# Block attention of a hybrid mixer, its units' scores and values' products issued in pairs

## What is computed

```python
u_conf, u_sc, u_att, u_lru = jnp.split(rms_norm(x, g) @ w_in, splits, axis=-1)
y_a = conformer_conv_mixer(u_conf, ...)   # depthwise convolution of 31 taps, group norm
y_b = short_conv_mixer(u_sc, ...)
y_c = moba_attention(u_att)               # block attention, the part that is reordered
y_d = rglru_mixer(u_lru, ...)             # convolution of 4 taps, two gates, a scan
y = jnp.concatenate([y_a, y_b, y_c, y_d], axis=-1) @ w_out
```

## Time and profile before

| | |
|---|---|
| time of three runs | 1281.03, 1281.20, 1281.74 us; median 1281.2 |
| profiled execution | 1281.13 us |
| its span on the core | 1279.3 us (1.8 us lie outside of it) |
| PE busy | 1271.2 us, 99% |
| DVE, ACT busy | 740.7 us (58%), 569.1 us (44%) |
| chain that ended last | PE 92%, DVE 4%, ACT 2% |

### The profile page before, as it was taken

One profiled execution on the slowest core, in us unless ns is written; L12 is line 12 of the kernel. 1 busy time (PEld: TensorE's weight loads), 2 busy tenths in 40 slices (PEclk: granted clock), 3 DMA queues, 4 the chain that ended last, 5 costly groups with the idle time before them and its releaser, 6 DMA issues.

```text
span 1279.3 us, 15979 instructions
## 1 busy us (share of the span) xinstructions
PE 1271.2 (99%) x6406; PEld 1065.5 (83%) x6406; DVE 740.7 (58%) x1091; ACT 569.1 (44%) x974; POOL 7.0 (1%) x8
## 2 busy tenths in 40 slices
PE   9999999999999999999999999999999999999998
PEld 9877898898888888888888898778898888888886
DVE  5779687575576555555633489777653433433333
ACT  4566554344446444444422364576442422322222
POOL 0000011000000000000000000000000000000000
PEclk9999999999999999999999999999999999999999
DMA  8445446222224233333433143123243333333311
GB/s 259 138 149 164 164 133 193 104 67 67 89 92 144 92 94 99 99 99 99 148 98 99 34 153 99 50 67 115 74 141 99 94 94 94 115 99 99 99 50 66
DMA packets 43521, 138.54 MB, mean 108 GB/s; under 512 B 4628, under 2 KB 10260, under 8 KB 43192
## 3 DMA queue, kind: packets, MB, share of 16 engines
q1 hardware_dynamic: 43016, 137.13, 34.2%
q10 hardware_dynamic: 432, 0.39, 0.1%
HBM read 131.74 MB, written 5.77 MB: 107 GB/s over the span
## 4 chain that ended last, share of the span: by engine, by line
PE 92%; DVE 4%; ACT 2%; DMA 1%; issue 1%; DVEq 0%; SPq 0%
PE bank L1285 16%; PE bank L1286 16%; PE bank L1287 16%; PE bank L1426 5%; PE bank L1427 5%; PE bank L1429 5%; PE bank L1430 5%; PE bank L1428 5%; PE bank L1431 5%; PE bank L1505 1%; DVE wlo L2153 1%; DVE R L2302 1%; PE bank L1357 1%; PE bank L1368 1%; DVE gb L2292 1%
## 5 line engine op out<-in xcount | busy, mean ns | idle before, releaser
L1285 PE MATMUL bank<-xh,whi 128*128 128x512 f32 (+1 forms) x1136 | 414.6, 365 | 1.0 <-DVE xl L2179 0.9
L1286 PE MATMUL bank<-xl,whi 128*128 128x512 f32 (+1 forms) x1136 | 409.9, 361 | 0.0
L1287 PE MATMUL bank<-xh,wlo 128*128 128x512 f32 (+1 forms) x1136 | 409.9, 361 | 0.0
L2153 DVE TENSOR_TENSOR wlo<-stage,whi 128x1024 fp32r<-128x1024 f32 (+1 forms) x222 | 267.4, 1210 | 227.9 <-ACT whi L1688 227.6
L1688 ACT CAST whi<-stage 128x1024 fp32r<-128x1024 f32 (+1 forms) x222 | 228.5, 1036 | 201.1 <-PE bank L1431 157.2
L1285 PEld LDWEIGHTS bank<-xh,whi 128*128 128x128 f32 x1136 | 214.4, 189 | 40.8 <-issue 7.0
L1287 PEld LDWEIGHTS bank<-xh,wlo 128*128 128x128 f32 x1136 | 214.4, 189 | 32.5
L1286 PEld LDWEIGHTS bank<-xl,whi 128*128 128x128 f32 x1136 | 214.5, 189 | 31.8 <-issue 0.2
L1426 PE MATMUL bank<-whi,xh 128*128 128x512 f32 x281 | 110.3, 393 | 0.1
L1427 PE MATMUL bank<-whi,xh 128*128 128x512 f32 x281 | 109.4, 389 | 0.0
L1431 PE MATMUL bank<-whi,xl 128*128 128x512 f32 x281 | 109.4, 389 | 0.0
(11 more groups left out here) (339 smaller groups left out, 1406.1 us busy)
## 6 DMA issues: line engine op xcount, KB each, us to landing
stage<-in_W_m SPq DMA_DIRECT2D x64, 512.0 KB, 3.6
stage<-in_W_up SPq DMA_DIRECT2D x44, 512.0 KB, 3.6
stage<-in_W_down SPq DMA_DIRECT2D x22, 512.0 KB, 3.6
stage<-in_W_in_a SPq DMA_DIRECT2D x19, 512.0 KB, 4.0
stage<-in_W_out SPq DMA_DIRECT2D x16, 512.0 KB, 3.7
stage<-in_W_in_b SPq DMA_DIRECT2D x10, 512.0 KB, 3.6
stage<-in_W_kv_k SPq DMA_DIRECT2D x8, 512.0 KB, 3.7
stage<-in_W_kv_v SPq DMA_DIRECT2D x8, 512.0 KB, 3.9
```

The costliest lines, as they stand in the source:

```text
L1285: e.matmul(b[:, cols], hi[:, k, :], xh[:, k, cols], start=(k == 0), stop=False)
L1286: e.matmul(b[:, cols], hi[:, k, :], xl[:, k, cols], start=False, stop=False)
L1287: last = e.matmul(b[:, cols], lo[:, k, :], xh[:, k, cols], start=False, stop=(k == 7))
L2153: e.tensor_tensor(wlo[:, plan.place[i], c], stage[:, i % NSTAGE, c], whi[:, plan.place[i], c].bitcast(F32), ALU.subtract).then_inc(S["w_lo"])
```

## The change

Units go in pairs (0 and 1, 2 and 3, 4 and 5, 6 and 7). `mb_scores(u)` issues the scores of u and u + 1 one behind the other; the values' products of a pair are issued together, directly ahead of the next pair's scores. The step that DVE and ACT shared under the name `mb_score` is two now, `mb_logit` (DVE) and `mb_exp` (ACT), so that they can stand at different places of the list. Each step of a pair has its own place: logits of u, logits of u + 1 with the exponential of u, reciprocal and scaling of u with the exponential of u + 1, turn of u with the scaling of u + 1, turn of u + 1, values' products. The taps are given out in other portions, 60 as before. No arithmetic is changed, and no instruction is added or removed. The core of the diff:

```diff
-    def mb_score(self, u):
-        for e in range(2):
-            self.fill("mb_score", u, e)
-            self.out(("mb_score", u, e), "mb_logit", 2 * u + e + 1)
-        self.step("mb_score", u)
+    def mb_scores(self, u):
+        for v in (u, u + 1):
+            for e in range(2):
+                self.fill("mb_score", v, e)
+                self.out(("mb_score", v, e), "mb_logit", 2 * v + e + 1)
+            self.step("mb_score", v)
+        self.step("mb_logit", u)
...
+        self.mb_pv(0)
+        self.mb_pv(1)
+        self.mb_scores(2)
+        tap(1)
+        yield
+        self.step("mb_logit", 3)
+        self.step("mb_exp", 2)
+        tap(3)
+        yield
+        self.step("mb_norm", 2)
+        self.step("mb_exp", 3)
+        tap(3)
+        yield
+        self.mb_turn(2)
+        self.step("mb_norm", 3)
+        tap(3)
+        yield
+        self.mb_turn(3)
+        tap(3)
+        yield
+
+        self.mb_pv(2)
+        self.mb_pv(3)
+        self.mb_scores(4)
+        tap(1)
+        yield
+        self.step("mb_logit", 5)
+        self.step("mb_exp", 4)
         tap(2)
         yield
+
+        self.step("mb_norm", 4)
+        self.step("mb_exp", 5)
+        self.lru_gates(0)
         tap(3)
         yield
...
+        self.mb_turn(4)
+        self.step("mb_norm", 5)
+        tap(3)
+        yield
+        self.mb_turn(5)
+        tap(3)
+        yield
+
+        self.mb_pv(4)
+        self.mb_pv(5)
+        self.mb_scores(6)
...
-            def mb_score(u):
+            def mb_exp(u):
...
-            def mb_score(u):
+            def mb_logit(u):
```

More of the change, by code:

```diff
@@ L813, in beside_mixer_two @@
         yield
-        self.mb_score(0)
+        self.mb_scores(0)
+        tap(1)
+        yield
+        self.step("mb_logit", 1)
+        self.step("mb_exp", 0)
         tap(2)
         yield
-        tap(3)
-        yield
         self.step("mb_norm", 0)
-        self.mb_score(1)
-        tap(2)
-        yield
+        self.step("mb_exp", 1)
         tap(3)
@@ L828, in beside_mixer_two @@
         self.step("mb_norm", 1)
-        self.mb_score(2)
-        tap(2)
+        tap(3)
         yield
+        self.mb_turn(1)
+        tap(3)
[7 more added lines that the diff above has]
+        self.step("mb_exp", 2)
         tap(3)
@@ L834, in beside_mixer_two @@
         self.step("mb_norm", 2)
[L835 to L838, removed]
+        self.step("mb_exp", 3)
+        tap(3)
         yield
-        tap(4)
+        self.mb_turn(2)
+        self.step("mb_norm", 3)
+        tap(3)
         yield
[L843 to L846, removed]
+        self.mb_turn(3)
[4 more added lines that the diff above has]
+        self.mb_scores(4)
+        tap(1)
+        yield
+        self.step("mb_logit", 5)
+        self.step("mb_exp", 4)
         tap(2)
@@ L849, in beside_mixer_two @@
         self.step("mb_norm", 4)
+        self.step("mb_exp", 5)
[4 more added lines that the diff above has]
+        self.step("mb_norm", 5)
+        tap(3)
+        yield
+        self.mb_turn(5)
+        tap(3)
+        yield
+        self.mb_pv(4)
+        self.mb_pv(5)
+        self.mb_scores(6)
         tap(1)
         yield
[L852 to L866, removed]
+        self.step("mb_logit", 7)
+        self.step("mb_exp", 6)
+        self.lru_gates(1)
         tap(3)
@@ L869, in beside_mixer_two @@
         self.step("mb_norm", 6)
-        self.mb_turn(5)
-        self.mb_pv(4)
-        self.mb_score(7)
+        self.step("mb_exp", 7)
         tap(3)
         yield
+        self.mb_turn(6)
+        self.step("mb_norm", 7)
+        self.step("lru_a")
         tap(3)
         yield
[L878 to L886, removed]
         self.mb_turn(7)
-        self.step("lru_a")
-        tap(4)
-        yield
         tap(60)
@@ L897, in beside_mixer_two @@
         yield
+        self.mb_pv(6)
         self.mb_pv(7)
@@ L2129, in _ @@
                         cf_var=cf_var, cf_exp=cf_exp, cf_gate=cf_gate, in2_a=in2_a, in2_v=in2_v,
-                        mb_score=mb_score, mb_norm=mb_norm, mb_turn=mb_turn, lru_in=lru_in, lru_gate=lru_gate,
+                        mb_exp=mb_exp, mb_norm=mb_norm, mb_turn=mb_turn, lru_in=lru_in, lru_gate=lru_gate,
                         lru_a=lru_a, lru_b=lru_b, lru_gelu=lru_gelu, sc_c=sc_c, sc_conv=sc_conv,
@@ L2704, in _ @@
                         last_norm=last_norm, cf_in=cf_in, cf_tap=cf_tap, cf_parts=cf_parts, cf_mean=cf_mean, cf_scale=cf_scale,
-                        cf_out=cf_out, mb_score=mb_score, mb_norm=mb_norm, mb_pv=mb_pv, lru_in=lru_in, lru_a=lru_a,
+                        cf_out=cf_out, mb_logit=mb_logit, mb_norm=mb_norm, mb_pv=mb_pv, lru_in=lru_in, lru_a=lru_a,
                         lru_b=lru_b, lru_scan=lru_scan, sc_x=sc_x, sc_conv=sc_conv, sc_b=sc_b, post_norm=post_norm,
```

## The result

The changed kernel takes 1282.85 us (median of 22 runs), the kernel before 1281.22 (22 runs beside them): ratio 1.0012, 95% interval 1.0007 to 1.0018. One run of the 22, at 1581 us and a mean granted clock of 0.75, stands apart and is left out of the ratio. The change costs 1.6 us, which is under the 0.2% that the prediction set for telling a change from none, though the interval excludes 1.

A forecast was written before the change was run, and what follows sets the result against it. PE, busy 99% of the span, was taken to bound the kernel. From 1281.13 us, 2.8 saved on stretches and waits of 2.8, 0.8 and 0.6 added gave 1282.5 us; range 1280.0 to 1284.9.

The forecast's parts named there:

- A: The forecast's own case: gain taken back by three waits, 1280.8 to 1283.7 us, no measurable change; chance 0.67.
- fewer stretches: Half-array stretches on PE in the block attention fall from twelve (5.3 us) to five (2.5 us), saving 2.8 us.
- idle ahead of unit 4's turn: PE asks at 21.4 us, but VectorE's queue delays unit 4's reciprocal and scaling until 24.1; PE waits 2.8 us.
- rival D: Granted clock falls to 1.2 GHz behind the idle; each 8 products cost 1.8 us more, 1284.3 us; chance 0.03.
- unit 5's turn: PE waits 0.8 us more there, because ACT needs 4.5 us after unit 4's scaling.
- values' products of unit 7: PE gets there in 9.4 us, ACT and DVE need 10.0 with `lru_a` in the path; wait 0.6 us.
- entering costs 0.09, and the product after the first full-array one comes 0.11 more than the pace: Border prices on PE at each half-array stretch, besides 0.20 us to leave scores or 0.15 to leave values' products.
- PE asks 3.6 us after unit 4's turn began: Step behind unit 5's wait: PE reaches unit 5's turn after 8 turns and 12 products, 3.6 us.
- The table load: The 1.28 us load moves from `lru_a` to ahead of unit 6's exponential, where ACT idles; no drain of 1.38 added.
- B: The waits are hidden and PE stays at 99% busy: 1278.3 us, faster; chance 0.08.
- C: Each hand-over between engines costs 0.1 us more and units with 0.4 us of cover wait too: 1284.9 us; chance 0.20.
- E: Neighbouring units' scores and products still cost a stretch's border each, so no saving while waits stay: 1285.3 us; chance 0.02.

The follow-up runs named there:

- e5: Kernel of e2 with ScalarE's and VectorE's `lru_a` moved behind unit 7's turn; 2.13 us below the kernel before, stage 77.34 us.
- e3: Changed kernel with nine extra, useless products on TensorE ahead of unit 4's turn, filling most of the idle; median 0.91 us above the kernel before.
- e7: Changed kernel with three extra, useless products ahead of unit 4's turn, filling part of the idle; median 1.91 us above the kernel before.
- e10: Changed kernel with one extra product ahead of unit 4's turn, waiting for unit 4's reciprocal, so the idle is cut in two; median 1.83 us above the kernel before.
- e2: Changed kernel with unit 4's and 5's reciprocals and scalings and unit 5's exponential ahead of the second convolution; 1.93 us under the kernel before.
- e1: Changed kernel with only unit 4's reciprocal and scaling moved ahead of the second convolution; median 1281.59 us, 0.47 above the kernel before.
- e8: The changed kernel run again, unaltered; median 1.59 us above the kernel before, stage 81.74 us.
- e4: Kernel before, twelve stretches, with unit 4's and 5's reciprocal and scaling moved behind the second convolution so that TensorE idles; 1286.45 us.
- e11: The kernel of e7 run again, unaltered; median 0.92 us above the kernel before, stage 80.85 us.
- e6: Kernel of e5 with one useless full-array product between the two units' scores of each pair; median 0.13 us above the kernel before, stage 78.99 us.
- e12: The kernel of e10 run again, unaltered; median 1.74 us above the kernel before, stage 80.80 us.

## Why the prediction was right, and where it was not

The time (1282.5 forecast, 1282.85 measured) and the case (A, no measurable change) came out. In the trace, in which the clock fell, the sum did so with one term missing and others too large:

| term | forecast, us | measured in the trace | from |
|---|---|---|---|
| fewer stretches | -2.8 | -2.5 | e5: -2.35, and 0.15 of wait in it |
| idle ahead of unit 4's turn | +2.8 | +2.6 | turn to turn against e5 |
| half clock behind it | 0 (rival D: +1.8) | +1.6 | products of the same chunk against e5 |
| unit 5's turn | +0.8 | 0 here, 0.65 at full clock | e3, e7, e10 |
| values' products of unit 7 | +0.6 | +0.3 here, 0.66 in e2 | 12 records |
| sum | +1.4 | +2.0 | stage: +2.03 |

The measured terms are differences to PE's timeline of e5 at the same instructions:

```profile
824.30 0.79 PE L1296 MATMUL bank<-xh,whi 128*128 128x512 f32 x1
...
827.44 1.03 PE L1650 MATMUL bank<-ident,R 128*128 128x128 f32 x8
828.23 0.48 PE L1296 MATMUL bank<-xh,whi 128*128 128x512 f32 x1
...
831.05 0.82 PE L1650 MATMUL bank<-ident,gb 128*128 128x128 f32 x6
```

Twelve products ahead of the turn take 3.14 us in e5 (824.30 to 827.44) and 5.75 in the changed kernel, up to 829.43: 2.61, of which the trace calls 2.45 idle. The twelve behind it take 2.82 (828.23 to 831.05) and 4.43 (830.27 to 834.70): 1.61, and the turn itself 0.05 more.

**What bounds the kernel: right.** PE waits for nobody before; the change could only save at borders and lose by waits. All three waits that the walk named exist, each at its place (unit 4's in the changed kernel, unit 5's in e1, e3 and e7, unit 7's in e2), and none at units 1 and 3 or ahead of `cf_mean`. At unit 7, where the walk left 0.4 us, e5 shows 0.1. The taps, subtractions and casts kept their order and cost nothing.

**The saving: right in kind, 0.3 us too large.** Sums of starts to next starts on PE in the stage, before and e5: scores 5.92 and 5.12 us, the four leavings of 0.20 exactly; values' products 5.57 and 4.97, four of 0.15 exactly; turns, gates and projection products together 68.20 and 67.25, 0.95 less, where the step "entering costs 0.09, and the product after the first full-array one comes 0.11 more than the pace", taken seven times, asked for 1.40. Of the 0.45 missing, 0.15 is the wait left in e5 ahead of unit 7's turn. 0.22 is a miscount of what was there before: the values' products of units 5 and 6 were left into a turn, and behind any turn the next product is late in any case. PE's timeline of the kernel before:

```profile
850.18 0.44 PE L1639 MATMUL bank<-ident,R 128*128 128x128 f32 x2
850.38 0.48 PE L1285 MATMUL bank<-xh,whi 128*128 128x512 f32 x1
850.70 0.39 PE L1286 MATMUL bank<-xl,whi 128*128 128x512 f32 x1
```

The step of 0.32 us from 850.38 to 850.70 stands behind turns in e5 too (no half array near), so the two stretches never paid 0.11 for it. The last 0.08 us are not traced. I had read the price off four stretches and multiplied by twelve; looking at each of the twelve for its neighbours would have given it.

**Unit 4's wait: right.** 2.8 foreseen, 2.45 to 2.6 measured. The walk of VectorE's queue gave 19.3 us for the span that ends in the reciprocal, and the trace has 19.3 (the subtraction starts at 808.68, the reciprocal ends at 828.01), in the order named and without a break.

**Units 5 and 7: right as waits, not in this kernel.** In the sum each stood as if PE ran at full clock. With the half clock PE came 1.6 us later and found unit 5 ready; the step "PE asks 3.6 us after unit 4's turn began" became 5.3. At full clock (e3) its chunk took 3.47 us for 2.82, 0.65 of the 0.8 (by the prediction's own terms, 4.5 less 3.6, it is 0.9). So the terms are not to be added to rival D but shared with it: A's unit 5 and D's clock exclude each other in part. Unit 7's wait depends in the same way on what PE has lost before it: 0.66 in e2, where PE had lost nothing, 0.27 in the changed kernel.

**The clock: this is the step that failed.** The sum takes the granted clock to stay at 1.00 behind the idle which the forecast itself makes. The prediction held the case D apart, with its price nearly right (1.8 us for eight products, measured 1.6) and its chance at 0.03, on the ground that no row shows an idle of this length. That no row shows it was ground for an open chance, not for a small one: by the mean clocks it came in some 15 of 32 executions or more. The Trainium skill (TensorE: Matmul & The Clock Gate, "Why this matters for your kernels") names idle gaps between bursts of matmuls as what brings half clock back; the changed kernel's row, 0.50 behind 2.45 us of idle, agrees, and so do e8 and e4. The number still landed, and in part by luck. In an execution with the fall, the clock's 1.6 us took the place of waits: units 5 and 7 cost 1.1 us less than foreseen and unit 4 0.2 less, against 0.3 less saved, so the account moved by 0.6 us in all, to +2.0. In one without it the forecast's own three waits are the account: an estimate from e3, e7 and e11, whose turn of unit 4 comes as late, is +1.1 us in the stage for the +1.4 foreseen. The median lies between the two.

**The table load: right.** It stands ahead of unit 6's exponential, and ScalarE then waits 1.07 us for VectorE all the same, so it is hidden. The gelu's load just ahead of it, on ScalarE's timeline of the changed kernel, shows what a load costs:

```profile
835.28 0.87 ACT L2041 COPY R<-bank 128x384 f32<-128x384 f32 x2 [0.65 <-PE bank L1650]
836.16 1.28 ACT L2080 ACT_TABLE_LOAD   x1
837.46 0.60 ACT L2080 ACTIVATE R<-bank 128x512 f32<-128x512 f32 x1
...
839.84 1.28 ACT L2021 ACT_TABLE_LOAD   x1
842.20 0.51 ACT L2021 ACTIVATE R<-R,st 128x256 f32<-128x256 f32 x1 [1.07 <-DVE st L2602]
```

The copies end at 836.15, the load starts at 836.16 and ends at 837.44, the next operation starts at 837.46: 1.30 us in all. The drain of 1.38 us that the Trainium skill (ScalarE: Activation LUTs, "What ACT_TABLE_LOAD costs") adds does not appear on either side of it, so the row's 1.28 was the right term.

**Rivals.** B: that 1278.3 can be had is nearly shown by e5 (1278.7), but only after four steps are moved. C: no unit but the three waits, and these come out as walked or shorter (2.6, 0.65 and 0.66 us for 2.8, 0.8 and 0.6), so an extra 0.1 us a hand-over does not show. E: refuted by e6.

## What to carry to other kernels

When work is grouped to save mode changes on the engine that bounds, every member of the group becomes ready as late as its last, and the feeding queues keep their old order: walk each queue up to the first consumer after the group, and move the group's short steps (here two reciprocals) ahead of long ones that nobody waits for yet (a convolution). Here that turned +1.6 us into -2.1 with the same instructions. Price an idle of the matrix engine as the idle plus what the clock may cost behind it, and look at the granted clock beside busy time, since at half clock the engine counts as busy. One trace is one execution: compare its mean clock with that of all timed ones before saying that the clock falls, or that it holds. And read a border's price at each place it occurs before multiplying it.

## What the runs showed of the hardware that was not expected

- Behind an unbroken idle of TensorE of 2.45, 2.44 and 3.17 us (traces of the changed kernel, e8, e4) the granted clock fell to 0.50, 1.2 GHz, and was back at 1.00 some 3 to 4 us later. It fell only about 1 us after the work had begun again (0.57 us of busy time in 829 to 830 still at 1.00), so that the turn itself ran at nearly full speed. In the traces behind 1.96, 1.76 and 1.76 us (e1, e7, e11), and behind 1.16 and 0.81 us with one product between (e10, e12), it stayed at 1.00.
- The same idle need not do the same in every execution. A mean clock of 0.998 or less, the sign of a fall in the stage, stands in 4 of 5 executions behind 3.17 us, in 15 of 32 behind 2.45, in 4 of 11 behind 1.96, in 5 of 22 behind 1.16 and 0.81, and in none of 22 behind 1.76. The traces also show that the clock doesn't fall at a fixed time into an idle: behind the last product of the program, whose work is the same in all of them, it fell after 2.0 us (e8), 2.3 (changed kernel), 3.6 (kernel before) and up to 5.0 (e1). What sets the time was not tried.
- In e10 and e12 the traces show the stage 0.9 us shorter than the changed kernel's, the timed runs none of it. Open, as said above.
